# The last plain unit of each feed-forward stage, moved in three parts between the products of the first pair

## The reference

```python
def _swiglu(x, w_in, w_out):
    gate, up = jnp.split(x @ w_in, 2, axis=-1)
    return (jax.nn.silu(gate) * up) @ w_out

x = x + 0.5 * _swiglu(_rmsnorm(x, n1_g[l]), ffn1_w_in[l], ffn1_w_out[l])
```

## Time and profile before

| | |
|---|---|
| median of three runs | 2025.37 us (2024.71 to 2025.46) |
| profiled execution, span from first to last instruction | 2022.9 us |
| PE busy | 2007.5 us, 99% of the span |
| DVE, ACT, POOL busy | 1273.5, 1064.1, 1124.2 us (63%, 53%, 56%) |
| mean granted TensorE clock | 0.999 of full speed |
| DMA | 206.19 MB, mean 102 GB/s |

### The profile page before, as it was taken

How to read it: one execution, slowest core, us unless ns; L and a number is a source line. 1 busy time by engine, 2 the same in 40 slices (tenths; PEclk the granted TensorE clock), 3 DMA queues, 4 the chain that set the end, 5 groups by cost and what they waited for, 6 DMA issues and landing times. The chain is left out here.

```text
span 2022.9 us, 33284 instructions
## 1 busy us (share of the span) xinstructions
PE 2007.5 (99%) x12322; PEld 1766.4 (87%) x12322; DVE 1273.5 (63%) x2245; ACT 1064.1 (53%) x1764; POOL 1124.2 (56%) x936
## 2 busy tenths in 40 slices
PE   9999999999999999999999999999999999999999
PEld 7998998777778889989988998998878778998997
DVE  7752765667762477626768763665688868742762
ACT  7642654344443456525656652564677766642651
POOL 2764775433333448746764765776323345764873
PEclk9999999999999999999999999999999999999999
DMA  4232323421221323332232333223344432332322
GB/s 171 95 110 89 112 96 117 138 84 64 73 74 52 100 79 115 110 110 84 95 109 80 115 103 106 94 92 120 115 131 129 128 107 76 112 106 84 113 95 96
DMA packets 69087, 206.19 MB, mean 102 GB/s; under 512 B 8448, under 2 KB 9472, under 8 KB 68928
## 3 DMA queue, kind: packets, MB, share of 16 engines
q1 hardware_dynamic: 67520, 201.29, 30.8%
q10 hardware_dynamic: 1408, 2.78, 0.4%
HBM read 189.49 MB, written 2.10 MB: 95 GB/s over the span
## 5 line engine op out<-in xcount | busy, mean ns | idle before, releaser
L624 POOL TENSOR_TENSOR w_lo<-raw,w_hi 128x512 fp32r<-128x512 f32 (+2 forms) x464 | 520.7, 1148 | 635.0 <-ACT w_hi L1255 473.3
L1255 ACT ACTIVATE w_hi<-raw 128x512 fp32r<-128x512 f32 (+2 forms) x472 | 358.8, 765 | 320.9 <-PE ps L701 253.8
L636 POOL TENSOR_TENSOR w_lo<-s,w_hi 128x512 fp32r<-128x512 f32 x234 | 312.3, 1336 | 190.3 <-ACT w_hi L1255 189.1
L777 PE MATMUL ps<-t_hi,w_hi 128*128 128x256 f32 x1248 | 354.3, 284 | 6.8 <-DVE scratch L1954 3.8
L779 PE MATMUL ps<-t_hi,w_lo 128*128 128x256 f32 x1248 | 353.9, 284 | 0.0
L778 PE MATMUL ps<-t_lo,w_hi 128*128 128x256 f32 x1248 | 353.9, 284 | 0.0
L636 POOL TENSOR_TENSOR w_lo<-raw,w_hi 128x512 fp32r<-128x512 f32 x234 | 302.6, 1306 | 58.6 <-ACT w_hi L1255 58.6
L777 PE MATMUL ps<-xn_hi,w_hi 128*128 128x256 f32 x936 | 265.1, 283 | 2.4 <-ACT scratch L1255 2.2
L778 PE MATMUL ps<-xn_lo,w_hi 128*128 128x256 f32 x936 | 264.9, 283 | 0.0
L779 PE MATMUL ps<-xn_hi,w_lo 128*128 128x256 f32 x936 | 264.8, 283 | 0.0
L699 PE MATMUL ps<-xn_hi,w_hi 128*128 128x512 f32 x648 | 258.7, 399 | 0.0
(11 more groups left out here) (260 smaller groups left out, 3759.3 us busy)
## 6 DMA issues: line engine op xcount, KB each, us to landing
raw<-weights SPq DMA_DIRECT2D x294, 512.0 KB, 3.3
raw<-weights SPq DMA_DIRECT2D x68, 256.0 KB, 2.7
raw<-weights SPq DMA_DIRECT2D x32, 384.0 KB, 3.0
k_hi_twice<-sb_k_hi SPq DMA_DIRECT2D x31, 128.0 KB, 2.3
k_lo_twice<-sb_k_lo SPq DMA_DIRECT2D x31, 128.0 KB, 2.3
x_sb<-x_t SPq DMA_DIRECT2D x8, 256.0 KB, 5.9
bias<-rel ACTq DMA_DIRECT2D x1, 2048.0 KB, 8.7
q_both<-sb_q_hi SPq DMA_DIRECT2D x16, 128.0 KB, 2.2
```

The lines of the kernel that those rows point to most:

```text
L624: last = nc.gpsimd.tensor_tensor(w_lo[s][:, k, :], raw[s][:, k, :], w_hi[s][:, k, :].bitcast(F32), ALU.subtract)
L636: nc.gpsimd.tensor_tensor(quad_of(n, i, w_lo), factor(n, F, i, raw, s_sum), quad_of(n, i, w_hi).bitcast(F32), ALU.subtract).then_inc(S["q_ ...
L777: pe.matmul(to, w[0][:, k, :], hi, start=opens, stop=False, skip_group_check=True)
L1255: return nc.scalar.activation(dst, src, ACT.Copy)
```

## The change

The last plain unit of every stage is taken from the end of `plain_tiles` and placed in three parts inside the first pair: behind product 1, behind product 6 and behind product 2. `LATE_AT` says where its eight weight blocks are cut: in stage 0 the parts are 0, 4 and 4 blocks, in the others 3, 2 and 3. The late unit's h is made later too: on DVE `plain_h` stands behind `add_p6` and `split_h` behind `gate_first`, on ACT `round_h` stands behind the rounding of quad 5 of the next tile. The queues of POOL and of the DMA issues keep their order.

```diff
+LATE_AT = [(0, 4), (3, 5), (3, 5), (3, 5)]
...
         def up_in_seven(n, c):
 
             first, end = seven_from(n, c), CHUNKS[c][1]
+
+            def late_plain(part):
+                if c == 0 and part[0] < part[1]:
+                    plain_unit(n, first - 1, 1, None, part)
+
+            at_5, at_2 = LATE_AT[n]
             for F in range(first, end):
...
                 product(n, F, 1)
+                if F == first:
+                    late_plain((0, at_5))
...
                 product(n, F, 6)
+                if F == first:
+                    late_plain((at_5, at_2))
                 pe.wait_ge(S["p1_copied"], p + 1)
                 product(n, F, 2)
                 if F > first:
                     pe.wait_ge(S["c22_made"], p)
                     product(n, F - 1, 3)
+                else:
+                    late_plain((at_2, UK))
                 pe.wait_ge(S["v1_made"], p + 1)
                 product(n, F, 7)
...
+        def plain_unit(n, F, g, waits=None, part=None):
+
+            u = up_unit(n, F, g)
+            unit(u, u % NSLOT, [plain_banks(n, F)[g]] * UK, xn, waits, part=part)
+
         def plain_tiles(n):
...
                 one(3, 0)
-                one(3, 1)
                 return
...
             one(1, 0, lambda k: means(FFN_STAT[n]) if k == MEAN_AT else None)
-            one(1, 1)
...
                 silu(0, 3)
-                round_h(0, 3)
                 return
...
             silu(n, 1)
-            round_h(n, 1)
...
                     round_7(n, F + 1, 5)
                 else:
                     round_down(n, c, 0)
+                if F == first and c == 0:
+                    round_h(n, F - 1)
                 round_7(n, F, 4)
...
             add_p6(n, F)
+            if F == first and c == 0:
+                plain_h(n, F - 1)
             if more:
                 sum_2(n, F + 1)
             gate_first(n, F)
+            if F == first and c == 0:
+                split_h(n, F - 1)
...
                 plain_gate(0, 3)
-                plain_h(0, 3)
-                split_h(0, 3)
...
                 plain_gate(n, 1)
-                plain_h(n, 1)
-                split_h(n, 1)
```

More of the change, by code:

```diff
@@ L840, in down @@
                  start=(e == 0), stop=(e == 1))
+        def plain_unit(n, F, g, waits=None, part=None):
+            u = up_unit(n, F, g)
+            unit(u, u % NSLOT, [plain_banks(n, F)[g]] * UK, xn, waits, part=part)
         def plain_tiles(n):
             def one(F, g, waits=None, part=None):
-                u = up_unit(n, F, g)
-                unit(u, u % NSLOT, [plain_banks(n, F)[g]] * UK, xn, waits, part=part)
+                plain_unit(n, F, g, waits, part)
             def first_mean(k):
```

## The result

The changed kernel takes 2048.56 us (median of four runs, 2045.93 to 2048.88), the kernel before 2025.16 us beside it: a ratio of 1.0113, 95% interval 1.0101 to 1.0126, or +23.4 us. The time lies inside the range on record, 6 us above its middle and 3.9 us above the sum of 2044.7. Three of the four runs (2048.31 to 2048.88 us, mean granted clock 0.991) lie at the 2048 us of rival (a); only the fourth (2045.93 us, 0.993) lies within the 2042 to 2047 us of the forecast itself.

The account below looks back on a forecast made before the run. TensorE, busy 99%, was taken as the bound. Later second-pair starts, including low clock after three long idle times, gave +15.9 us; low clock behind half the new stops +3.4: 2025.4 + 19.3 = 2044.7 us, forecast 2042 to 2047, range 2035 to 2050.

Parts of the forecast that it names:

- rival (a): Every new stop before the second pair is followed by the low clock: +22.7 us, 2048 us; chance 0.12.
- the two clock terms: Low clock: 1.7 us after each of three long idle times, and 3.4 us behind the four new stops.
- The starts of product 1: Start times stay, so TensorE idles 5.7, 4.95 and 4.1 us ahead of product 1 in stages 0, 2, 3; none in 1.
- Rival (e): The change wins: product 1's inputs are ready when TensorE arrives, also in stages 0, 2, 3; -4.0 us, 2021 us; chance 0.06.
- From product 1 to product 7: First pair: four products and the late unit take 11.16 us without further wait, plus 1.7 us low clock after long idle times.
- The new wait: Second pair's product 1 waits for VectorE's scaling, starting 3.63 us after product 7 in each stage; TensorE idles 2.04 us.
- rival (c): The stop before the second pair does not come, VectorE or ScalarE reaching the scaling otherwise: +7.7 us, 2033 us; chance 0.07.
- (d): Both (b) and (c), the late unit only swapping the place of its cover: +2.6 us, 2028 us, no change; chance 0.05.
- The clock behind the new stops: Half of the four stops before the second pairs bring the low clock: 2 x 1.7 = 3.4 us, bounds 0 and 6.8.
- Rival (b): The clock never falls at the new places: +10.8 us, 2036 us; chance 0.10.
- The price of 1.7 us: Loss charged per low-clock stretch, from the kernel before, stage 2: clock averaging 0.66 over 5 us after a 2.01 us stop.
- one stop costs more than its length: Claim that the 2.01 us stop in stage 2 also brought the low clock, 1.7 us lost.

Follow-up runs that it names:

- e2: Changed kernel with the late unit's matmuls all ahead of product 1 again, the late h left where the change puts it: 2027.45 us, ratio 1.0012.
- e1: Changed kernel with VectorE's scaling put ahead of making the late h, and ScalarE's rounding of it behind copy_a: 2033.56 us, ratio 1.0043.
- e4: Changed kernel with extra matmuls, results unused, in the long idle times ahead of product 1 in stages 0, 2 and 3: 2041.29 us, ratio 1.0083.
- e6: Changed kernel with the edits of e1 and e4 together: 2028.52 us, ratio 1.0017.
- e5: The change in stage 1 alone, stages 0, 2 and 3 as in the kernel before: 2028.35 us, ratio 1.0016.
- e3: Changed kernel with the edits of e1 and e2 together: 2020.77 us, ratio 0.9979 to the kernel before.
- e8: e7 with the late unit of stage 2 cut, five blocks ahead of product 1 and three behind it: 2017.52 us, ratio 0.9963.
- e7: e3 with add_p6 of the first pair also ahead of sums s1 and s3 of the second pair: 2018.59 us, ratio 0.9967.

## Why the prediction was right

The path was right, step by step, and the time lies in the range; the two clock terms were too small, and the time came out at the 2048 us of rival (a), which had a chance of 0.12, rather than at the forecast's 2042 to 2047.

**The starts of product 1.** The step holds as it was put. Idle times of 5.51, 4.84 and 3.98 us were measured for 5.7, 4.95 and 4.1, and none in stage 1; the difference is mostly the end of the last matmul, which the forecast did not take off. e2 shows that the missing cover makes them. Rival (e) falls by the rows of DVE and POOL above: the preparation ran no faster with the late unit out of the way.

**From product 1 to product 7.** 11.16 us without the clock were put; stage 1 took 768.14 - 756.82 = 11.32, the others 13.17, 13.23 and 13.60. So the low clock cost 2.0 to 2.4 us there, not 1.7, if the 0.16 us of stage 1 are counted with it. That is +1.4 us over the three stages.

**The new wait.** 3.63 us from product 7 to the second pair, measured 3.65 in all four stages; 2.04 us idle, measured 2.06. It came in every stage, so rival (c) falls, and with it (d); e1 takes it away, which shows the chain that makes it.

**The clock behind the new stops: the mis-sized term.** Half of the four stops were taken to be followed by the low clock, 3.4 us. In the profiled execution all four were, 6.8 us, which is rival (a) for that execution. With the 1.4 us above, 19.3 + 3.4 + 1.4 = 24.1 us stands against 23.9 in the span. How many of the four it was is chance: none in the profiled run of e4, and the run of the changed kernel at 2045.93 us, with its higher mean clock, probably had fewer. Rival (b) falls by the windows, in which all seven stops were followed by the low clock, and by e6 against e1, where keeping PE at work in the three long ones takes 5.0 us off.

The price of 1.7 us was taken from a place where it cost nothing. In the earlier trace rows the clock lost 1.7 us, but product 7 stops right behind for 1.15 us all the same, so the row does not show that "one stop costs more than its length". That the price held behind the new stops is in part luck; there the waits of PE show no further stop in the products that could take up the slower matmuls. In e5 the two groups of runs lie 1.5 us apart by their medians (2028.68 and 2027.17 us).

Of the 2.5 us between the span and the median, 2.0 are start and end: that much lies between time and span of one and the same run (2048.8 and 2046.8 us). So the profiled execution of the kernel before took some 2024.9 us, 0.5 us less than the median; the forecast of the difference does not hang on it.

By the experiments the 23.4 us are, in round numbers, 3.6 for the late unit's place less what the late h made later wins (e6: 7.7 against e3, less 4.2), 5.0 for the clock behind it (e1 less e6), 8.9 for the four stops (4 x 2.22 us of PE's start-to-start time, from 3.65 less product 7's 1.43) and the rest, some 6, for the clock behind these.

One part of the change is a gain that the prediction names (a make, a round and a split of the late h no longer stand ahead of the copy) but does not price by itself: the late h made later takes the rounding of h, with its wait of 0.82 us for DVE in the earlier trace rows, out of ACT's queue ahead of product 1's copy. It is worth 4.2 us where it is not set ahead of the scaling and the late unit stays where it was (e3).

## What to carry to other kernels

A piece of work that fills stops further on may be the cover of something earlier: ask first how soon the next instruction could start without it, from the end of what it waits for, and only then what it fills. When a late result is moved in an in-order queue, follow what stands behind its first waiting instruction on every engine it passes through; here one product on VectorE held a rounding and a copy on ScalarE, which held a sum and a scaling on VectorE, which held TensorE. And where idle time can't be avoided, two short pieces can be cheaper than one that brings the low clock (e8 against e7, 1.1 us).

## What the runs showed of the hardware

A low clock ahead of a stop can be free. The kernel before has runs with a mean granted clock of 0.999 and of 1.000, and they take the same time (2024.49 to 2025.54 us and 2024.76 to 2025.51 us, 19 runs), although has 1.7 us of clock lost in stage 2. Product 7 stops there anyhow:

```profile
1108.99 0.39 PE L777 MATMUL ps<-t_hi,w_hi 128*128 128x256 f32 x1 [1.15 <-DVE scratch L1954]
```

In e2 and e3 (the rows beside e3) the same place is seen with the clock up and with the clock low, and product 7 comes 5.78 and 5.88 us after product 5. When e7 took that stop away, the same low clock cost about a microsecond (its runs above).

The same idle time of 2.06 us, at the same place of the program, was followed by the low clock in the profiled execution of the changed kernel (0.79 over 8 us, four times) and not in that of e4 (1.00, four times); the mean clocks and times of the runs of e4 suggest that it differs between executions of one program too. The Trainium skill ("TensorE: Matmul & The Clock Gate", Part 1) says of the start of a kernel that the number of slow matmuls there is run-variable. No run here compares the starts of kernels; behind stops inside one, the four runs of e4 differ as well, by up to 4.5 us. Idle times up to 1.62 us, the longest of the new stops of e2, left the clock up in its profiled execution, and 2.00 us in e3 and e7 did not; one idle time of 2.00 us in e2 (its third row) left it up as well. So the runs here give no single length of idle time behind which the clock falls.

The fall does not come at the same moment either. Behind the stop of 2.06 us in stage 0 of the changed kernel PE goes on at 68.49 with 0.12 us from one matmul to the next, and slows down to 0.21 us only when it is at work again:

```profile
68.95 0.28 PE L778 MATMUL ps<-xn_hi,w_hi 128*128 128x256 f32 x1
69.07 0.28 PE L779 MATMUL ps<-xn_lo,w_hi 128*128 128x256 f32 x1
...
69.76 0.42 PE L778 MATMUL ps<-xn_hi,w_hi 128*128 128x256 f32 x1
69.97 0.41 PE L779 MATMUL ps<-xn_lo,w_hi 128*128 128x256 f32 x1
```

Behind the 5.51 us ahead of product 1 the first matmul is slow already (0.55 us in its row above).
